# One decoder step on one Trainium2 core: compression and prompt attention in one block, first scores issued behind the last mixing product, compressed tiles turned without waiting for heads

## The reference, cut to what matters

```
def compress_one(rows, w1, w2, pe):          # rows (b, t, 2 groups, 64)
    proj = einsum('bnsgd,rsdh->rbngh', rows in blocks of 16, w1)
    hid = pe_term + proj[0, :, 0:nc] + proj[1, :, 1:1 + nc]
    return gelu(hid) @ w2                    # once for keys, once for values

# prompt, per block of 128 queries, 8 heads in 2 groups of 4
p = masked_softmax(q @ kc^T);  o_cmp = p @ vc
p = masked_softmax(q @ ks^T);  o_slc = p @ vs    # 16 blocks of 64: all are selected
p = masked_softmax(q @ kw^T);  o_win = p @ vw    # window of 512
o = g0 * o_cmp + g1 * o_slc + g2 * o_win
```

## Time and profile before

| | us |
|---|---|
| runs | 2256.99, 2257.52, 2258.82 |
| the profiled execution's own time | 2256.94 |
| its span, first to last instruction | 2254.9 |
| PE busy | 2145.1 (95%) |
| DVE busy | 1185.3 (53%) |
| ACT busy | 670.1 (30%) |
| POOL busy | 587.8 (26%) |
| compression, about | 248 to 365 |
| prompt attention, about | 365 to 672 |

### The profile page before, as it was taken

The page is one execution under the profiler, slowest core; times in us unless marked ns, Lnnn a source line. Parts: engine busy times, 40 slices in busy tenths (PEclk is TensorE's granted clock), DMA queues, the critical chain, the costliest instruction groups (busy, mean ns, idle before and its releaser), DMA issues.

```text
span 2254.9 us, 34331 instructions
## 1 busy us (share of the span) xinstructions
PE 2145.1 (95%) x13481; PEld 1959.5 (87%) x13481; DVE 1185.3 (53%) x2155; ACT 670.1 (30%) x1407; POOL 587.8 (26%) x367
## 2 busy tenths in 40 slices
PE   8999997998879999999999999999999999999999
PEld 3798785666666699999999999989999999999998
DVE  5774374888877247765210333464454444554445
ACT  3332364776664034332111212331101011010112
POOL 0112112544552045552000113422212022211220
PEclk9999897999999899999999999999999999999999
DMA  9021353000016322221333444212111111111112
GB/s 363 14 97 36 107 174 121 1 1 1 1 57 227 108 59 54 58 58 47 87 84 85 150 132 106 75 40 75 38 57 38 53 42 40 55 38 57 38 38 78
DMA packets 175589, 168.62 MB, mean 75 GB/s; under 512 B 10194, under 2 KB 156083, under 8 KB 170116
## 3 DMA queue, kind: packets, MB, share of 16 engines
q1 hardware_dynamic: 167462, 117.96, 17.6%
q0 software_dynamic: 7760, 48.55, 6.6%
q10 hardware_dynamic: 224, 0.08, 0.0%
HBM read 152.98 MB, written 17.87 MB: 76 GB/s over the span
## 4 chain that ended last, share of the span: by engine, by line
PE 61%; DVE 2%; issue 1%; POOL 0%; ACT 0%; POOLq 0%; ACTq 0%
PE psall L244 19%; PE psall L246 18%; PE psall L245 18%; PE psall L2376 2%; PE psall L2011 2%; DVE work L2257 1%; PE psall L2038 1%; DVE work L2562 1%; DVE work_short L2574 0%; POOL work L1933 0%; PE psall L2053 0%; PE psall L2020 0%; PE psall L3112 0%; PE psall L2046 0%; PE psall L2055 0%
## 5 line engine op out<-in xcount | busy, mean ns | idle before, releaser
L244 PE MATMUL psall<-hT_short,ring_short 128*128 128x344 f32 x1896 | 614.7, 324 | 6.3 <-DVE ring_short L239 3.4
L246 PE MATMUL psall<-hT_short,ring_short 128*128 128x344 f32 x1896 | 607.4, 320 | 0.0
L239 POOL TENSOR_TENSOR ring_short<-ring,ring_short 128x1024 fp32r<-128x1024 f32 (+3 forms) x52 | 196.9, 3786 | 1068.3 <-DVE ring_short L234 756.8
L245 PE MATMUL psall<-work_short,ring_short 128*128 128x344 f32 x1392 | 445.3, 320 | 0.0
L244 PEld LDWEIGHTS psall<-hT_short,ring_short 128*128 128x128 f32 x1896 | 358.5, 189 | 7.3 <-issue 6.2
L246 PEld LDWEIGHTS psall<-hT_short,ring_short 128*128 128x128 f32 x1896 | 358.2, 189 | 0.0
L245 PEld LDWEIGHTS psall<-work_short,ring_short 128*128 128x128 f32 x1392 | 262.2, 188 | 0.2
L3273 DVE SCALAR_TENSOR_TENSOR xT<-psall,mod,xT 128x344 f32<-128x344 f32 (+1 forms) x264 | 151.3, 573 | 133.2 <-PE psall L246 129.4
L245 PE MATMUL psall<-xT_short,ring_short 128*128 128x344 f32 x648 | 208.4, 322 | 0.0
L3153 ACT ACTIVATE work<-psall 128x344 f32<-128x344 f32 (+1 forms) x66 | 30.0, 456 | 504.3 <-PE psall L246 503.2
L244 PE MATMUL psall<-work_short,work_short 128*128 128x344 f32 x528 | 176.5, 334 | 3.5 <-POOL work_short L239 2.9
(11 more groups left out here) (452 smaller groups left out, 4020.0 us busy)
## 6 DMA issues: line engine op xcount, KB each, us to landing
ring<-in_w_up SPq DMA_DIRECT2D x44, 512.0 KB, 5.0
ring<-in_w_in SPq DMA_DIRECT2D x27, 512.0 KB, 3.8
work<-in_ada_w SPq DMA_DIRECT2D x23, 512.0 KB, 4.2
work<-in_w_down SPq DMA_DIRECT2D x10, 1024.0 KB, 4.9
ring<-in_ada_w SPq DMA_DIRECT2D x9, 512.0 KB, 4.4
x_spill<-xT SPq DMA_DIRECT2D x4, 1032.0 KB, 15.0
xT<-x_spill SPq DMA_DIRECT2D x4, 1032.0 KB, 6.3
ring<-in_ada_w SPq DMA_DIRECT2D x4, 1024.0 KB, 14.9
```

The costliest lines, as they stand in the source:

```text
L239: return eng.tensor_tensor(lo, src, hi, ALU.subtract)
L244: pe.matmul(out, w[0], x[0], start=first, stop=False)
L245: pe.matmul(out, w[0], x[1], start=False, stop=False)
L246: return pe.matmul(out, w[1], x[0], start=False, stop=last)
```

## The change

The compression becomes a set of engine programs that are called at the head of the attention's block, so that there is one block and one meeting less, and the clearing of old semaphores stands ahead of the compression. The order of its parts changes in these places:

- PE issues the scores of items 0 and 1 (`EARLY` = 2) directly behind the last mixing product, ahead of the last two `make`; DVE takes their maxima ahead of the last two `place`.
- Pair 0 has query buffers of its own (in the room of `rope` and `gain`, and in `spare`). POOL splits it behind the last indirect transfer, ACT and DVE ahead of their last `second`. Pair 1 waits on POOL for the last mixing product.
- The first mask goes to `ring` 6144 as soon as the selected keys are split (`k_high`), and DVE converts it ahead of the last `second`. The second mask is loaded once the last turn of the compression is done.
- Each engine's order at the attention's head: `begins` of units 0 and 1 is no longer held up by `freed` = 0, and unit 1 gets `RAMP` = 2 tiles more of lead. From the first tile of unit 0 on, PE's list was scores 0 to 3, turn 0, turn 1, scores 4, scores 5, turn 2, weigh 0, scores 6, turn 3; it becomes scores 0 to 3, turn 0, scores 4, turn 1, scores 5, scores 6, turn 2, scores 7, weigh 0, scores 8, turn 3. DVE's was maxima 0 to 3, then reciprocals 0 to 3; it becomes maxima 0 to 2, reciprocal 0, maximum 3, reciprocals 1 to 3. From item 9 on the lists are the same.
- `turn` of a compressed tile waits only for the compressed probabilities; in the first tile of keys of every unit each head's transpose waits for that head alone.

```diff
-    s.rope = sb("rope", [P, TT + 1, 32], F32)
-    s.gain = sb("gain", [P, 4, HD], F32)
+    small, s.small_short = region("small", (TT + 1) * 32 + 4 * HD)
+    s.rope, s.gain = view(small, 0, TT + 1, 32), view(small, (TT + 1) * 32, 4, HD)
...
-def stage_compress(nc, s, T, splits, inputs):
+def compress_programs(s, T, splits, inputs):
...
+        if before:
+            before()
         second(NB, 1, NSUB_S)
+        if between:
+            between()
         third(NB, 0, NSUB_S)
         third(NB, 1, NSUB_S)
...
+    first_q = [s.small_short(0, HPG, P), s.spare_short(0, HPG, P)]
+    q_parts = lambda p: q_split[p % 2] if p else first_q
-    cmp_add_f = view(s.ring, 0, TT, HD)
+    cmp_add_f = view(s.ring, 6144, TT, HD)
+    EARLY = 2
...
-    LOOK, SPACE, LEAST, SPARE = 4.0, 1.0, 0.5, 2.0
+    LOOK, SPACE, LEAST, SPARE, RAMP = 4.0, 1.0, 0.5, 2.0, 2.0
...
-        p = max(u.first - LOOK - later * SPACE, begins[-1] + LEAST if begins else -LOOK * HPG, u.freed - SPARE)
-        begins.append(max(min(p, u.first - 0.1 + 0.0001 * i), u.freed - 0.9))
+        ahead = LOOK + RAMP if u.index == 1 else LOOK
+        p = max(u.first - ahead - later * SPACE, begins[-1] + LEAST if begins else -LOOK * HPG, u.freed - SPARE)
+        p = min(p, u.first - 0.1 + 0.0001 * i)
+        begins.append(max(p, u.freed - 0.9) if u.freed else p)
...
-            sp.dma_start(cmp_add_f, T["c_cmp_add"]).then_inc(masks_in, 16)
-            sp.dma_start(cmp_mul, T["c_cmp_mul"]).then_inc(masks_in, 16)
+            compress.sync(sp)
+            sp.wait_ge(k_high, 2)
+            sp.dma_start(cmp_add_f, T["c_cmp_add"]).then_inc(add_in, 16)
+            sp.wait_ge(compress.turned, compress.TURNED)
+            sp.dma_start(cmp_mul, T["c_cmp_mul"]).then_inc(mul_in, 16)
...
+                elif p:
+                    pool.wait_ge(compress.mixed, compress.MIXED)
...
             def turn(i):
-                if i == u.first:
-                    pe.wait_ge(normed, HPG * (u.index + 1))
+                if i == 0:
+                    pe.wait_ge(compress.placed, compress.PLACED)
...
                     for j in range(HPG):
+                        if c == u.lo:
+                            pe.wait_ge(normed, HPG * u.index + j + 1)
...
+            def first_scores():
+                pe.wait_ge(k_high, 2)
+                for i in range(EARLY):
+                    scores(i)
+            compress.tensor(pe, first_scores)
             pe.wait_ge(mask_cast, 1)
-            pe.wait_ge(k_high, 2)
...
+                if u.index == 1 and j == 0:
+                    act.wait_ge(compress.made, compress.MIXED)
+                    act.wait_ge(mask_cast, 1)
...
-            queries(0)
+            compress.scalar(act, lambda: queries(0))
             queries(1)
+            act.wait_ge(compress.placed, compress.PLACED)
             act.activation(vc_short[0:NC_P, :, 1, :], ...)
-            act.wait_ge(mask_cast, 1)
...
+            def prepare():
+                queries(0)
+                v.wait_ge(add_in, 16)
+                v.tensor_copy(cmp_add, cmp_add_f).then_inc(mask_cast, 1)
+            def first_maxima():
+                for i in range(EARLY):
+                    maximum(i)
+            compress.vector(v, prepare, first_maxima)
             queries(1)
-            v.wait_ge(masks_in, 32)
-            v.tensor_copy(cmp_add, cmp_add_f).then_inc(mask_cast, 1)
```

More of the change, by code:

```diff
@@ L841, in stage_compress, with pipeline @@
     pe_terms, pe_read = s.sem("c_pe_terms"), s.sem("c_pe_read")
-    def pipeline(eng, first, second, third):
+    def pipeline(eng, first, second, third, before=None, between=None):
         first(0, 0, NSUB_P)
@@ new lines, in sync, with gpsimd @@
+    def sync(sp):
+        for i in range(3):
+            sp.dma_start(w2[0:HD, i, :], T["cmp_w2"][0, i // 2]).then_inc(w2_in, 16)
+    def gpsimd(pool):
+        splits.round_keys(pool, 0)
+        pool.wait_ge(splits.k_round, 4)
+        pool.wait_ge(inputs.idx_ready, 1)
+        for b in range(NB):
+            for a, src in enumerate((T["cache_cmp_k"], T["cache_cmp_v"])):
+                pool.wait_ge(turned, 4 * (2 * b + a) + 4)
+                pool.indirect_dma_start(
+                    out=rows[a].rearrange("p t c -> p (t c)"), out_offset=None,
+                    in_=src[0].rearrange("n (j t) g d -> (n j) (t g d)", t=CMP_STRIDE),
+                    in_offset=bass.IndirectOffsetOnAxis(ap=s.gidx[:, b:b + 1], axis=0)).then_inc(rows_in[a], 16)
@@ new lines, in evacuate, with run @@
+    def evacuate(eng, copy, done, banks):
+        def run(q, a, n):
+            wait(eng, mixed, 2 * q + a - 1)
+            for bank in banks:
+                eng.wait_ge(turned, 4 * (2 * q + a) + bank + 1)
+                src = view(s.ps[bank], 0, 2, 2, P)
+                for s2 in range(2):
+                    for g in range(NG):
+                        last = copy(pairs[a][s2 * HD:(s2 + 1) * HD, g, 2 * bank:2 * bank + 2, 0:n],
+                                    src[g * HD:(g + 1) * HD, :, s2, 0:n])
+                last.then_inc(done, 1)
+        return run
@@ new lines, in scalar, with lift_gelu @@
+    def scalar(act, before):
+        act.wait_ge(pe_terms, 1)
+        def lift_gelu(q, a, n):
+            m = n - 1
+            act.wait_ge(mixed, 2 * q + a + 1)
+            wait(act, summed, 2 * q + a - 1)
+            src = view(s.ps[4 + a], 0, NG, P)
+            act.activation(lifted[a][0:HD, :, 0:m], src[HD:P, :, 1:n], ACT.Identity,
+                           bias=pe_h[0:HD, a:a + 1]).then_inc(lift, 1)
+            act.wait_ge(summed, 2 * q + a + 1)
+            wait(act, made, 2 * q + a - 1)
+            act.activation(act_h[a][0:HD, :, 0:m], hid[a][0:HD, :, 0:m], ACT.Gelu_apprx_tanh).then_inc(gelu, 1)
+        act.wait_ge(pe_read, 2)
+        splits.place_keys(act, 0, 1)
+        pipeline(act, evacuate(act, lambda o, i: act.activation(o, i, ACT.Copy), evac_a, (1, 3)), lift_gelu, nothing,
+                 before=before)
```

218 lines of the change are left out of this document (92 added, 126 removed).

## The result

| | us |
|---|---|
| before, median of 4 runs on the same chip (range) | 2258.17 (2256.99 to 2259.29) |
| changed, median of 4 runs (range) | 2227.28 (2225.39 to 2228.51) |
| ratio, 95% interval | 0.9875 (0.9853 to 0.9898) |
| forecast, its range | 2234.9 (2226 to 2248) |
| profiled span, before and changed | 2254.9 and 2226.6 |

The kernel became faster: the two medians differ by 30.9 us, the recorded ratio of 0.9875 (1.25%) stands for 28, and the two profiled spans differ by 28.3, which is what the traces can explain. The forecast was 22 us and the time lies inside the range, near its fast end.

What follows compares the result with a forecast made beforehand. PE was taken as the bound, busy 2145.1 of 2254.9 us (95%). The seam's 9.0 and the compressed tiles' 13.0 make 22 us: 2256.9 - 22.0 = 2234.9 us, range 2226 to 2248.

Steps and rivals of the forecast that it cites:

- The seam: Last mixing product to tile 0's transposes: query split and mask conversion leave the path; 9.0 us saved, bounds 7.0 and 10.5.
- Behind the seam: After tile 0's transposes, until 403.50 us: PE is the limit, its clock may gain or lose; taken as nothing, bounds +4 and -4.
- The compressed tiles: Turns of compressed tiles no longer wait for POOL's normalisation; 13 us saved, between 3 and 23.
- What decides is DVE: At compressed tiles, DVE's 12.0 us idle before their low parts sets the gain, against PE's 23.0; 1 added for long stops.
- The example stop: PE stops at 558.31, turns the compressed tile at 561.05; 2.75 us of work fits in, so nearly the whole stop goes.
- Idle time before L1636 up by a few us: Sign at the turns of heads' tiles on PE: idle time there was to rise by a few us.
- The bound of 6: Sign: PE's idle time from POOL before compressed tiles below 6 us instead of 23.0; DVE's before their low parts below 4.
- Head-wise waits: First tile of keys of each unit, turned head by head: 0.7 us at most in the first tile, a fraction elsewhere.
- Rival C: PE's view right and clock recovers earlier: compressed tiles worth 20, 3 more behind the seam; 2224.9 us, chance 0.12.
- B: Compressed tiles' stop returns one tile later or as a wait for DVE: worth 3, time 2244.9 us, chance 0.20.
- D: Around 400 us PE's fill thins and its clock stays at 0.50: 40 us lost, time 2275, chance 0.04.
- The table load: ACT's load before the first exponent: a rule's drain of about 1380 ns, gain 1.4 us less, 2236.3; left out.

Runs made afterwards that it cites:

- experiment 9: Changed kernel with scores and maxima of items 0 and 1 behind the last `make` and `place` instead of ahead; median 2227.29 us, ratio 0.9868.
- experiment 10: Changed kernel with the exponents' table loaded behind the last gelu and exponents 0 and 1 ahead of ACT's wait for the placed rows; 2225.32 us, ratio 0.9858.
- experiment 4: Changed kernel with the old rules for `begins` (units 0 and 1 held up by `freed` = 0, no `RAMP`); median 2226.18 us, ratio 0.9860.
- experiment 3: Changed kernel, but each unit's first tile of keys waits for all four heads at once; median 2230.49 us, ratio 0.9883.
- The pads: Small memsets on DVE ahead of each tile's low part: changed kernel with two 2225.74, four 2226.07, eight 2234.50 us; kernel before with two 2255.51 us.

## Why the prediction came out right, and where it was off

**The seam: right, in size and in steps.** I had 9.0; the last transpose of tile 0 against the first one before came 24.4 - 16.3 = 8.1 earlier, and 0.7 for the three others makes 8.8. First exponent: 7.6 expected, 8.1 measured. POOL's start: 373.7, that is 10.8 behind the last mixing product's end, and it was 10.9. I had held up to 1 us back for scores 2 and 3 at the lower clock. They took 372.38 to 376.5, 4.1 instead of 3.0, and through the reciprocal of head 1 this cost POOL 0.65. The wait that the change adds (both `place` behind two maxima) I had seen; that it eats the whole gain of the early scores I had not said, and experiments 9 and 10 show it. Neither the scores' place (experiment 9) nor the new order (experiment 4) gives anything of the seam's gain. What is left is the queries and the mask that left the path, and the meeting of the engines that went. For these the timeline speaks: scores 0 started 9.05 us behind the last mixing product's end before, waiting for L1783, and 2.0 us behind it in experiment 9. They were not undone one by one.

**Behind the seam: nothing, as taken.** The first compressed tile came 7.9 us earlier, 0.9 less than tile 0's last transpose, although its own stop of 0.8 had gone. The clock in stretches of 5 us, PE alone, of the changed kernel:

```profile
365.00:370.00 5.00, 3.29 (x19) 1.00 0.31 105
370.00:375.00 5.00, 2.62 (x7) 0.64 0.94 314
375.00:380.00 5.00, 2.42 (x7) 0.50 1.00 392
380.00:385.00 5.00, 3.94 (x24) 0.50 0.08 28
385.00:390.00 5.00, 5.00 (x26) 0.65 0.02 3
390.00:395.00 5.00, 3.31 (x20) 1.00 0.00 0
```

From 390 on it was at the higher level, where it had been at the lower one before. But in the same 5 us PE was busy for only 3.31: it stood for 1.97 us until 395.39, and for 0.55 until 397.97, for DVE's low parts. In the whole seam section PE's idle time before heads' tiles that DVE's low parts ended rose from 0.3 to 2.5 us. So what the clock gave was waited away.

**The compressed tiles: right mechanism, mis-sized term.** The step that failed is "What decides is DVE". I took DVE's 12.0 plus 1, between 3 and 23; the tile section became 19.5 shorter, and 16.6 of that are the compressed tiles' wait (experiment 3). The example stop of my own text had shown that nearly the whole stop goes on PE, and I then cut the sum to half by the row of another engine. That row was no bound: 12.0 is DVE's idle time before one shape of one of its steps. Over the tile section DVE stood idle for 262.10 - 218.22 = 43.9 us, and of that 17.1 went, about as much as of PE's. The pads show that ten more microseconds of work fit in even after the change. The 19.5 are 19.7 of stops gone, less 1.4 that came back before heads' tiles and 1.8 before scores, and 3.0 of PE's busy time. "Idle time before L1636 up by a few us" was too much: 1.4 in the tile section. The bound of 6 for the compressed row was right (2.6), and so was that of 4 for DVE's (0.4).

**Head-wise waits: under-priced.** I said 0.7 in the first tile and a fraction elsewhere. They were worth 0.8 in tile 0, against 0.7 expected, and up to 1.9 in the seam section; over the other tiles they were worth 2.9, not a fraction of a microsecond. That is PE's idle time before heads' tiles, 3.0 us more in experiment 3.

**Rival C** (PE's view right, and the clock) gave 20 for the second half and is the one that came true in this part; 3 us of PE's busy time, with more of the higher clock, are there too, but in the tile section and not right behind the seam. In B the stop would have come back a tile later or as a wait for DVE: PE's idle time that DVE ended before heads' tiles rose by 2.2, against 19.7 that went. D did not occur; the clock over the tile section rose from 0.97 to 0.99.

**The table load.** It started 0.02 us behind an activation's end and the exponent followed 0.01 behind the load (369.45 + 0.31, 369.78 + 1.28, 371.07); in experiment 10, right behind the gelu, the distances are 0.01 and 0.02. By the Trainium skill, "ScalarE: Activation LUTs", section "What ACT_TABLE_LOAD costs", a drain of some 1380 ns comes with the load at every switch of tables. No row here shows it, on either side of the load, and leaving it out was right.

**Clearing semaphores, transfers, later stages** were taken at nothing. Behind decode the two spans differ by 0.3. The clearing now stands ahead of the seam section, which begins at 363.2 us on average in the ten changed kernels and at 362.3 in the three built on the kernel before; with a scatter of several microseconds this neither shows nor excludes the 1.0 that I had allowed for it.

## What to carry to other kernels

What follows is drawn from this one kernel. When a stop of the bounding engine goes, look at what that engine has queued behind it (one example stop, followed in the timeline) and price the stop by that engine's own row; another engine at 84% bounds it only where its queue shows no idle time left in the same few microseconds. Idle time listed before one shape is not an engine's room; take the length of the stretch less its busy time. And where a step is moved ahead, look for what it pushes back on the next engine: here the first scores early, with their maxima ahead of the rows that the exponents wait for, gave nothing, and the seam became shorter once the exponents were moved too. And count idle time within the same stage on both sides: a window that reaches past the stage's end takes in stops of the next one.

## What the runs showed of the hardware

The mask's conversion on DVE (128x512, f32 to bf16) took 1.38 us before and 0.43 after. Before, it began at 370.49 while POOL's subtraction ran from 369.82 to 371.59, and ended at 371.87, 0.28 behind it. In the changed kernel, and in experiment 10 (0.43 as well), POOL did nothing beside it. POOL's subtraction took 1.76 when DVE's of the same operand shape began with it, and 1.29 when none did. Rows of the kernel before, then one of the changed kernel:

```profile
367.26 0.69 DVE L1732 TENSOR_TENSOR work_short<-work,work_short 64x512 fp32r<-64x512 f32 x1 [1.95 <-POOL work_short L1537]
367.31 1.76 POOL L1539 TENSOR_TENSOR work_short<-work,work_short 64x512 fp32r<-64x512 f32 x1
...
366.04 1.29 POOL L1557 TENSOR_TENSOR work_short<-work,work_short 64x512 fp32r<-64x512 f32 x1
```

The Trainium skill, "SBUF — State Buffer", section "SBUF: two separate sides", says that DVE, in a two-port mode or with two SBUF inputs beside a GpSimd operation that reads SBUF, and GpSimd take a shared port pair from each other: the one that starts first has it for its whole instruction, and the other is blocked. The rows agree for both engines; that the conversion runs in a two-port mode no row says. I had costed this conversion with 1.38 under cover, so the sum did not depend on it.

A pause of 4.09 us before scores 2, behind a thin stretch, came with the lower clock for scores 2 and 3 (0.77 us for the first product), a pause of 0.94 with the higher one (0.47): in this seam the longer wait cost more than its own length.
